# Opening of a two-layer diffusion trunk: the first modulation columns by column tiles, the scale first, and the small rows issued by ScalarE's queue

## What is computed

```python
    for i in range(DEPTH):
        m = jnp.split((sc @ w_mod[i] + b_mod[i])[:, None, :], N_MOD, axis=-1)
        mc = jnp.split((scc @ w_mod[i] + b_mod[i])[None, None, :], N_MOD, axis=-1)
        h = h + 0.5 * m[2] * _swiglu(_modulate(_rmsnorm(h, ffn1_norm[i]), m[0], m[1]),
                                     ffn1_w1[i], ffn1_w3[i], ffn1_w2[i])
...
def _rmsnorm(x, g):
    y = xf * lax.rsqrt(jnp.mean(xf * xf, axis=-1, keepdims=True) + EPS)
...
def _modulate(n, shift, scale):
    return n * (1.0 + scale) + shift
```

## Time and profile before

| | us |
|---|---|
| three runs | 2978.53, 2972.64, 2977.95 |
| their median | 2977.95 |
| the profiled execution | 2978.58 |
| its span, first to last instruction | 2976.8 |
| first row of products (line 690) starts | 64.87 |
| unit (1, 0) starts | 83.86 |
| unit (1, 1) starts | 93.59 |

### The profile page before, as it was taken

One profiled execution on the slowest core, in us unless ns is written; L12 is line 12 of the kernel. 1 busy time (PEld: TensorE's weight loads), 2 busy tenths in 40 slices (PEclk: granted clock), 3 DMA queues, 4 the chain that ended last, 5 costly groups with the idle time before them and its releaser, 6 DMA issues.

```text
span 2976.8 us, 43751 instructions
## 1 busy us (share of the span) xinstructions
PE 2895.1 (97%) x16914; PEld 2473.9 (83%) x16914; DVE 1661.0 (56%) x3086; ACT 890.2 (30%) x1389; POOL 104.9 (4%) x82
## 2 busy tenths in 40 slices
PE   7999999999989999999999999999999999999998
PEld 3888888888756788888888888888888757898996
DVE  3877578743366568766777335443433466543443
ACT  4221122233346442211222322122233256422222
POOL 0000000024000000000000000000024000000000
PEclk9999999999999999999999999999999999999999
DMA  5434343422300033433442123222222300233232
GB/s 200 127 120 132 94 127 122 125 55 65 88 1 1 22 99 121 131 108 113 129 128 89 57 63 113 67 61 63 68 71 65 81 1 1 78 92 99 85 101 69
DMA packets 422727, 255.39 MB, mean 86 GB/s; under 512 B 25985, under 2 KB 418025, under 8 KB 422634
## 3 DMA queue, kind: packets, MB, share of 16 engines
q1 hardware_dynamic: 422634, 254.13, 28.7%
HBM read 252.01 MB, written 2.10 MB: 85 GB/s over the span
## 4 chain that ended last, share of the span: by engine, by line
PE 93%; DVE 2%; ACT 2%; issue 1%; DMA 1%; SPq 0%; DVEq 0%; ACTq 0%
PE pair L690 55%; PE pair L686 26%; PE pair L886 2%; PE pair L934 2%; PE pair L646 2%; PE pair L902 1%; PE pair L596 1%; PE pair L911 1%; PE pair L862 1%; ACT buf L1196 1%; PE pair L844 1%; PE pair L919 1%; DMA pro_w<-in_w_mod 0%; DVE n_lo L1355 0%; DVE lo_w L1316 0%
## 5 line engine op out<-in xcount | busy, mean ns | idle before, releaser
L690 PE MATMUL pair<-n_hi,hi_w 128*128 128x258 f32 (+2 forms) x3456 | 851.0, 327 | 14.2 <-DVE n_lo L1355 8.7
L690 PE MATMUL pair<-n_lo,hi_w 128*128 128x258 f32 (+2 forms) x3456 | 847.8, 326 | 0.0
L690 PE MATMUL pair<-n_hi,lo_w 128*128 128x258 f32 (+2 forms) x3456 | 847.4, 326 | 0.0
L690 PEld LDWEIGHTS pair<-n_hi,hi_w 128*128 128x128 f32 x3456 | 538.9, 191 | 74.7 <-issue 10.3
L690 PEld LDWEIGHTS pair<-n_lo,hi_w 128*128 128x128 f32 x3456 | 539.2, 191 | 56.6
L690 PEld LDWEIGHTS pair<-n_hi,lo_w 128*128 128x128 f32 x3456 | 539.1, 191 | 56.1
L1316 DVE TENSOR_TENSOR lo_w<-raw_w,hi_w 128x1024 fp32r<-128x1024 f32 (+1 forms) x296 | 396.7, 1340 | 307.5 <-ACT hi_w L1004 306.7
L1004 ACT CAST hi_w<-raw_w 128x1024 fp32r<-128x1024 f32 (+1 forms) x296 | 328.7, 1111 | 671.6 <-PE pair L690 378.4
L1476 DVE SCALAR_TENSOR_TENSOR mod_acc<-mod_w,silu_c,mod_acc 128x256 f32<-128x256 f32 x896 | 364.6, 478 | 0.0
L1399 DVE TENSOR_TENSOR buf<-pair,rstd 128x512 f32<-128x512 f32 (+1 forms) x308 | 164.7, 570 | 319.1 <-PE pair L690 319.1
L686 PE MATMUL pair<-h_hi,hi_w 128*128 128x512 f32 x1232 | 338.7, 345 | 0.0
(11 more groups left out here) (182 smaller groups left out, 2088.1 us busy)
## 6 DMA issues: line engine op xcount, KB each, us to landing
raw_w<-in_ffn_w SPq DMA_DIRECT2D x176, 512.0 KB, 3.8
mod_w<-in_w_mod SPq DMA_DIRECT2D x64, 1024.0 KB, 5.1
raw_w<-in_ffn_w SPq DMA_DIRECT2D x64, 704.0 KB, 4.6
raw_w<-in_w_in SPq DMA_DIRECT2D x38, 512.0 KB, 3.9
pro_w<-in_w_mod SPq DMA_DIRECT2D x2, 4096.0 KB, 18.5
raw_w<-in_w_out SPq DMA_DIRECT2D x16, 512.0 KB, 4.0
x_tok<-in_x SPq DMA_DIRECT2D x4, 512.0 KB, 5.2
out<-x_tok SPq DMA_DIRECT2D x4, 512.0 KB, 2.7
```

The lines of the kernel that those rows point to most:

```text
L690: mm = pe.matmul(pair[s][:, a:a + m], wt[:, k * P:(k + 1) * P], src[:, of(k):of(k) + m], start=opens, stop=closes)
```

## The change

The two rows of the modulation are computed and used apart, the scale first:

- `first_mod` is called first for the scale (`pro_scale`). It uses column tiles: contraction tiles k and k + 4 go to output partitions 32j to 32j + 31 with j = k mod 4, by a stationary operand of 32 columns (`silu_wide`, two columns of values and 30 of zeros). The four partial sums are added when the row is turned into columns, by a product with `fold` (line 605 of the changed kernel) in place of the transposes. The copy out of PSUM is of 128 partitions, 1024 columns.
- Each 4 MB block is loaded in two halves with a semaphore each. The block of the shift is issued behind the first `raw_w`.
- `opening_pair` takes the place of `first_pair` for the first sweep. It issues only the streams of 512 columns (part 0) of both units, with `first_mod` of the shift between its rows; then the columns of the shift, the sum of squares, and only then the second streams (part 1).
- The adds to the sum of squares, the lambdas and the exponential are moved: three adds ahead of the scale, four between the tiles of `low`, the lambdas behind the last `low` and behind `mod_add`.
- In all sweeps that start from `n_hi`, the shift's low part stands in `n_hi` beside the high part: the second streams have 260, 256 and 258 columns in place of three of 258, and the bias is the sum of two pairs of PSUM columns (a `tensor_reduce` in place of a copy).
- The eighteen small transfers (seventeen rows and the lambdas) and the four of `fold` are issued by ScalarE, at the head of its program, in place of SyncE. No ScalarE-issued transfer exists in the kernel before.

The diff, cut:

```diff
-        x_tok, pro_w2, c_rows, rows, lam_row = overlay(("x_tok", (TOK // P) * D, F32), ("pro_w2", KD * D, F32),
-                                               ("c_rows", P, F32),
-                                               ("rows", 3 * P, F32), ("lam_row", DEPTH * 4 * DDIM, F32))
-        lam_prod = sq[0]
+        x_tok, pro_shift, c_rows, rows, lam_row, silu_wide = overlay(
+            ("x_tok", (TOK // P) * D, F32), ("pro_shift", KD * D, F32), ("c_rows", P, F32), ("rows", 3 * P, F32),
+            ("lam_row", DEPTH * 4 * DDIM, F32), ("silu_wide", KD * 32, F32))
+        mod_rows = [x_tok[:, m * D:(m + 1) * D] for m in range(2)]
+        lam_prod = x_tok[:, 2 * D:2 * D + TOK]
...
+        def streams(w, s, extra):
             lead = 0 if w["ctx"][s] else CTX
-            return ((lead, BLK - lead, lambda k: k * BLK + lead), (BLK, 258, lambda k: KD * BLK + k * TAIL))
-        def shift_cols(tensor):
-            return tensor[:, KD * BLK:KD * BLK + KD * TAIL].rearrange("p (k c) -> p k c", c=TAIL)[:, :, 256:258]
+            return ((lead, BLK - lead, lambda k: k * BLK + lead), (BLK, 256 + extra, lambda k: KD * BLK + k * TAIL))
+        def shift_cols(part):
+            return n_hi[:, KD * BLK:KD * BLK + KD * TAIL].rearrange("p (k c) -> p k c", c=TAIL)\
+                [:, :, 256 + 2 * part:258 + 2 * part]
...
                 sp.dma_start(x_tok[:, a * D:(a + 1) * D], src).then_inc(x_full, 16)
-            for L in range(DEPTH):
-                small(rows[0:UNITS_MOD, L * P:(L + 1) * P], as_rows(t["b_mod"][L]))
...
-            for g in range(4):
-                sp.dma_start(fold[32 * g:32 * (g + 1), :], t["k_ident"][0:32, 0:32]).then_inc(fold_full, 16)
-            wm = t["w_mod"][0].rearrange("(k p) c -> p k c", p=P)
-            for m, dst in enumerate((pro_w1, pro_w2)):
-                sp.dma_start(dst[:, :].rearrange("p (k c) -> p k c", k=KD), wm[:, :, m * D:(m + 1) * D])\
-                  .then_inc(pro_full[m], 16)
+            def load_first_mod(m, dst):
+                wm = t["w_mod"][0].rearrange("(k p) c -> p k c", p=P)
+                for k in range(0, KD, KD // 2):
+                    sp.dma_start(dst[:, k * D:(k + KD // 2) * D].rearrange("p (k c) -> p k c", c=D),
+                                 wm[:, k:k + KD // 2, m * D:(m + 1) * D]).then_inc(pro_full[m][k // (KD // 2)], 16)
+            load_first_mod(1, pro_scale)
...
+                if q == 0:
+                    load_first_mod(0, pro_shift)
...
             def first_mod(m, src):
                 pe.wait_ge(silu_ready, 2)
-                pe.wait_ge(pro_full[m], 16)
-                for a in range(0, D, 512):
-                    for k in range(KD):
-                        mm = pe.matmul(pair[m][0:2, a:a + 512], silu_c[:, 2 * k:2 * k + 2],
-                                       src[:, k * D + a:k * D + a + 512], start=(k == 0), stop=(k == KD - 1))
+                for r in range(2):
+                    pe.wait_ge(pro_full[m][r], 16)
+                    for a in range(0, D, 512):
+                        for j in range(4):
+                            k = 4 * r + j
+                            mm = pe.matmul(pair[2][32 * j:32 * (j + 1), a:a + 512], silu_wide[:, 32 * k:32 * (k + 1)],
+                                           src[:, k * D + a:k * D + a + 512], start=(r == 0), stop=(r == 1))
                 mm.then_inc(mrow_done, 1)
-            def mod_columns():
-                for m in range(2):
-                    pe.wait_ge(mrow_out[m], 1)
-                    for u in range(m * KD, (m + 1) * KD):
-                        mm = pe.transpose(pair[2][:, 2 * u:2 * u + 2], mod_rows[0:2, u * P:(u + 1) * P], ident[0:2, 0:2])
+            def mod_columns(m):
+                pe.wait_ge(fold_full, 16 * 4)
+                pe.wait_ge(mrow_out[m], 1)
+                for u in range(KD):
+                    mm = pe.matmul(pair[2][:, 2 * u:2 * u + 2], mod_rows[m][:, u * P:(u + 1) * P], fold[:, 0:2],
+                                   start=True, stop=True)
                 mm.then_inc(mod_done, 1)
...
-                        for a, m, of in streams(w, s):
+                        for n, (a, m, of) in enumerate(streams(w, s, 0 if src is src_lo else 2 if wt is lo else 4)):
+                            if part not in (None, n):
+                                continue
                             mm = pe.matmul(pair[s][:, a:a + m], wt[:, k * P:(k + 1) * P],
                                            src[:, of(k):of(k) + m], start=opens, stop=closes)
-                if k == w["kt"] - 1:
+                if k == w["kt"] - 1 and part != 0:
                     mm.then_inc(unit_done[s], 1)
...
+            def opening_pair(w):
+                open_slot(w, 0, 0, True)
+                for n in range(KD + LAG):
+                    if n < KD:
+                        pe.wait_ge(n_ready, n + 1)
+                        row(w, n, 0, 0)
+                    if n == LAG:
+                        open_slot(w, 0, 1, True)
+                    if n == KD - 2:
+                        pe.wait_ge(mod_out, 1)
+                        first_mod(0, pro_shift)
+                    if n >= LAG:
+                        row(w, n - LAG, 1, 0)
+                mod_columns(0)
+                pe.wait_ge(cols_out, 1)
+                sum_stream(norm_width(w))
+                pe.wait_ge(shift_ready, 1)
+                for s in range(2):
+                    for k in range(KD):
+                        row(w, k, s, 1)
...
-                        pe.wait_ge(cols_out, 1)
-                        first_mod(0, pro_w1)
-                        sum_stream(norm_width(w))
-                        first_mod(1, pro_w2)
-                        mod_columns()
+                        first_mod(1, pro_scale)
+                        mod_columns(1)
...
         def _(act):
+            def small(dst, src):
+                act.dma_start(dst, src).then_inc(small_full, 16)
+            for L in range(DEPTH):
...
+            small(rows[G_FINAL:G_ROWS, 2 * P:3 * P], as_rows(t["final_norm"]))
+            small(lam_row[0:1, :], t["diff_lambda"].rearrange("l a d -> (l a d)").rearrange("(o n) -> o n", o=1))
+            for g in range(4):
+                act.dma_start(fold[32 * g:32 * (g + 1), :], t["k_ident"][0:32, 0:32]).then_inc(fold_full, 16)
             act.wait_ge(c_done, 1)
             for e in range(2):
-                act.activation(silu_c[:, e:2 * KD:2], pair[2][:, e * KD:(e + 1) * KD], ACT.Silu).then_inc(silu_ready, 1)
+                act.activation(silu_c[:, e:2 * KD:2], pair[2][:, e * KD:(e + 1) * KD], ACT.Silu)
+                if e == 0:
+                    act.wait_ge(wide_zero, 1)
+                act.activation(silu_wide[:, e:32 * KD:32], pair[2][:, e * KD:(e + 1) * KD], ACT.Silu).then_inc(silu_ready, 1)
             for k in range(0, KD, 2):
                 act.wait_ge(xt_done, k + 1)
                 act.copy(tile(x, k), pair[0][:, 0:TOK]).then_inc(xt_out[0], 1)
-            act.wait_ge(lam_ready, 1)
-            act.activation(lam_exp[:, :], lam_sum[:, :], ACT.Exp).then_inc(lam_ready, 1)
...
+                    elif w["base"] == 0:
+                        high(0, w_cols)
+                        high(1, w_cols)
+                        split_hi(w, 0, 1, True)
+                        for k in range(2, KD):
+                            high(k, w_cols)
+                            if k in (3, 4, 5):
+                                square_x((k + 2) // 2, k % 2, TOK)
+                        act.wait_ge(mrow_done, 2)
+                        act.copy(mod_rows[0], pair[2][:, :]).then_inc(mrow_out[0], 1)
+                        act.wait_ge(mod_out, 2)
+                        shift_high(w)
+                        cnt["n"] += KD
                     else:
                         split_hi(w, 0, 1, True)
                 cnt["x"] += 1
                 act.wait_ge(xsum_done, cnt["x"])
                 std(pair[3], w_cols, D)
                 if w is not None and w["base"] == 0:
-                    act.wait_ge(mrow_done, 1)
-                    act.copy(mod_rows[0:2, 0:D], pair[0][0:2, :]).then_inc(mrow_out[0], 1)
-                    shift_high(w)
-                    for k in range(KD):
-                        high(k, w_cols)
-                    cnt["n"] += KD
+                    act.wait_ge(lam_ready, 1)
+                    act.activation(lam_exp[:, :], lam_sum[:, :], ACT.Exp).then_inc(lam_ready, 1)
...
+            def first_columns(m):
+                dve.wait_ge(mod_done, 2 - m)
+                for e in range(2):
+                    ins = dve.tensor_tensor(mod[:, 2 * m * KD + e:2 * (m + 1) * KD:2], pair[2][:, e:2 * KD:2],
+                                            b_mod[:, m * KD:(m + 1) * KD], ALU.add)
+                ins.then_inc(mod_out, 1)
...
-                    for k in range(KD - 1):
+                    for k in range(3):
                         add_x(k // 2, k % 2, TOK)
+                    dve.wait_ge(mrow_done, 1)
```

(29 more changed lines are left out.)

89 lines of the change are left out of this document (47 added, 42 removed).

## The result

| | before | changed |
|---|---|---|
| median of the runs side by side, us | 2978.24 (2972.64 to 2978.78, 4 runs) | 2946.16 (2945.97 to 2947.07, 4 runs) |
| profiled execution, us (its span) | 2978.58 (2976.8) | 2947.07 (2945.3) |
| first products start | 64.87 | 33.05 |
| unit (1, 0) starts | 83.86 | 67.41 |
| unit (1, 1) starts | 93.59 | 77.50 |

The ratio is 0.9897, with a 95% interval of 0.988 to 0.9914: 32 us less, where 16 to 17 were forecast. The first thing to read is at which point of the program the 32 us are won. At unit (1, 1), behind which I had assumed that nothing changes, the gain is 93.59 - 77.50 = 16.1 us, which is the forecast's 16.7 within 0.6. The other 16 us come later.

A forecast was written before the change was run, and what follows sets the result against it. TensorE, busy 2895 of 2977 us, was taken as the bound, so gains lie where it waits or does other work. The gain of 18.2 at unit (1, 1) less 1.5 for the clock is 16.7: 2962 us, range 2954 to 2970.

The forecast's parts named there:

- Supply: Opening transfers: scale's first half issued at 4.9 instead of 12.57, landed at 23.1; later blocks not waited for; tokens charged 0.7 us.
- The scale and the shift: Opening, both first_mod calls: 3.5 us each with four column tiles side by side, then the turn into columns, step 0.65.
- the pessimistic bound from the earlier trace: Weak overlap of column tiles in first_mod: 8.7 us per call, from four 44-column products in the trace of the kernel before.
- The first tiles and VectorE: Opening: VectorE paces the first tiles, 15.0 us, last at 46.2; later its low weights open unit (1, 0) at 66.0.
- The new wait: TensorE idle 2.3 us ahead of unit (1, 0), waiting for VectorE's low weights.
- The clock: Opening: a 1.2 GHz stretch of TensorE, mostly under VectorE's pace; charged 1.5 us, bounds 0 and 4.
- The queue change: Small transfers issued by ScalarE: 0.5 us of waiting saved, less 0.7 charged for small packets; at most 2.5 us.
- Everywhere else: Behind the opening: widths 260, 256, 258 count as three times 258; bias reduction 0 overall, at most 0.3 us in the opening.
- Serial column tiles: Rival: first_mod calls stay at 13.9 us, 2981 (with late rows 0.08); at the low clock 2998 (0.05).
- slow issues on ScalarE: Rival: opening transfers cost 1 us each to issue, token copies 10 us later, 2971; chance 0.07 together with weak overlap.
- late rows: Rival: small rows arrive late in the opening, 2964 or 2977; chance 0.08 for 2973 to 2984, together with serial tiles.
- The low clock: Rival: shift's first_mod and first tiles at low clock throughout, 9.1 becomes 12.5, 2964 to 2966; no chance of its own.

## Why the prediction was wrong, point by point

**Supply.** Right. The scale's block was issued at 4.97 (forecast 4.9), the engines were full in the stretch that had been thin, and neither `raw_w`, nor the shift's block, nor the first `mod_w` was waited for. ScalarE's transfers ended at 8.98 (8.5), with 3.8 us of cover left. The first transposes began 0.24 us later than before; I had charged 0.7, and small transfers on SyncE's queue gave 13.20, so nothing of it can be put down to ScalarE's queue. The small rows were through at 22.7, not 23.9.

**The scale and the shift.** `first_mod` at 3.5 was 3.64 twice, near full overlap of four; the pessimistic bound from the earlier trace rows was 8.7. The turn into columns I priced at the old step's 0.65; it took 1.92 and 1.84, for eight products (16 records) whose stationary operand is now 128 x 128 in place of 2 x 128. This term was too low by 1.2 us twice on the path, and only the first of the two cancelled against the small rows.

**The first tiles and VectorE.** The last `low` ended at 45.8 (46.2), the shift's columns began at 54.73 (54.4), unit (1, 0) at 67.41 after a wait of 2.41 (66.0 after 2.3). The new wait was named with its cause, and it is there.

**The clock.** The charge of 1.5 was right in size and wrong in place, so its agreement is luck. From 24 to 44 the granted clock was 0.75 and then 0.52, and it lay under VectorE's pace, as argued. What was paid came behind the wait ahead of (1, 0): from 67.41 to 77.50 are 10.1 us, where 24 weights at 0.353 are 8.5. That the sum came within 0.6 us at (1, 1) owes something to errors that cancel: the turns into columns took 2.4 us more in all, and the tokens and small rows 1.2 less.

**The queue change.** I put it at 0.5 us of waiting less 0.7, and at most 2.5. It is 3.1 us in the opening and 1.3 in the whole. The second half of the block is there at 26.18, as forecast (26.16), but it is wanted 0.7 earlier than I had it, and the low clock that lasts 4 us longer was not in the sum.

**Everywhere else: the step that failed.** "From there on the program is the same in both kernels" is not so: the widths and the bias change in every sweep that starts from `n_hi`. "260, 256 and 258 columns are as many as three times 258" is true and says nothing of the time. I had priced the edit at 0 by counting columns, and the only size that I considered was the reduction of the bias, which indeed costs no more than the copy (0.15 us). It was worth 15 us by the periods, and 17.5 by the medians of the kernels with and without it. The trace of before held the hint: two rows of it, 83.50 and 83.86, put a weight with 770 columns at 0.353 us, which is 0.032 more than its columns at 2.4 GHz. A tenth of these products' time was in something that I had no name for, and an edit that touched all of them was given neither a bound above nor one below. A quarter of that 0.032 for 3 x 1288 weights, a share that I choose now and that no row gives, would be 31 us either way. By their periods the kernels lie between 30.7 us less (256 three times) and 3.1 more (the swapped order) than with 258 three times. So there was much to win and little to lose, and no row of before told that either.

**The rivals.** Serial column tiles, slow issues on ScalarE and late rows did not occur. The low clock did cover the first tiles, up to 43.3, but neither call of `first_mod` (3.64 both). The chance of faster was rightly high, the range was too narrow, for it took in only the bounds of the opening.

## What to carry to other kernels

An edit that touches every product of the inner loop has to be bounded by the part of the loop's period that columns do not explain, also where the number of columns stays the same; read the period from start to start, not from busy time. Then time a few widths and orders of the inner loop, since they are cheap edits and can be worth as much as a restructured opening. Issue column tiles in turn, not one after another, and if a wait of TensorE is shortened, look for the clock behind it: part of the gain can be there.

## What the chip showed that I had not expected

- Period of three weights with 512 + second stream: 1040.0 ns with second streams of 256, 1060.0 with 258 and with 264, 1057.7 with 260, so 1.9% for 0.3% more columns. In layer 1, with a first stream of 256: 708.2 with 256, 719.9 with 258, 723.3 with 264.
- The order 260, 256, 258 takes 1050.5 ns, the order 260, 258, 256, with the weights loaded in another order too, takes 1062.4.
- A weight with streams of 512 and 258 takes 353.3 ns, one with 512 and 256 takes 346.7. The Trainium skill, page "TensorE: Matmul & The Clock Gate", section "Back-to-back issue gap", gives N / 2.4 + 2.5 ns for the warm gap of a single isolated product and says that in a stream it over-counts at large N. By that formula the first would take 326 ns, an estimate from the page. The traces do not agree: here the formula under-counts, by 27 ns.
- A period can have more than one steady value in the same program: 1053.4 ns in some sweeps and 1047 in others of the changed kernel, each held through the sweep.
- Four column tiles of 32 columns, 512 moving columns of float32: 3.64 us for 16 products in turn, 8.83 tile by tile, against 13.89 for the old 16 products without column tiles.
- In ten kernels TensorE waited 2.3 to 2.5 us ahead of unit (1, 0). In nine the low clock followed, until about 71 us in the changed kernel, where it cost 1.6 us more; in one (2.39 us of waiting) it did not. Behind the one wait of 0.96 us it did not either.
